# Loading a per-layer input with features on partitions by single-element DMA transfers from ScalarE's queue, in place of row loads and TensorE transposes

## What is computed

```python
for i in range(DEPTH):                      # DEPTH = 2
    f = swiglu(rmsnorm(h, g[0]), ffn_w_gate[i, 0], ffn_w_up[i, 0], ffn_w_down[i, 0])
    h = h + FFN_RES_WEIGHT * rmsnorm(f, g[1])
    m = retention(...) if i == 0 else stick_breaking(...)
    h = h + rmsnorm(m, g[3])
    f = swiglu(rmsnorm(h, g[4]), ffn_w_gate[i, 1], ffn_w_up[i, 1], ffn_w_down[i, 1])
    h = h + FFN_RES_WEIGHT * rmsnorm(f, g[5])
    gate = jax.nn.sigmoid(rmsnorm(h, g[6]) @ ple_w_gate[i])
    e = p[i] @ ple_w_proj[i]                # p[i]: (1, 256 tokens, 256 features)
    h = h + rmsnorm(gate * e, g[7])
```

## Time and profile before

| | us |
|---|---|
| Median of 3 runs | 1379.35 (1378.95 to 1379.9) |
| Span of the profiled execution | 1377.3 |
| TensorE busy | 1368.1 (99%) |
| VectorE busy | 940.4 (68%) |
| ScalarE busy | 724.2 (53%) |
| GpSimd busy | 121.1 (9%) |
| DMA engines, mean | 56.4% for SyncE's queue |

### The profile page before, as it was taken

One profiled execution on the slowest core, in us unless ns is written; L12 is line 12 of the kernel. 1 busy time (PEld: TensorE's weight loads), 2 busy tenths in 40 slices (PEclk: granted clock), 3 DMA queues, 4 the chain that ended last, 5 costly groups with the idle time before them and its releaser, 6 DMA issues.

```text
span 1377.3 us, 19699 instructions
## 1 busy us (share of the span) xinstructions
PE 1368.1 (99%) x6928; PEld 1156.3 (84%) x6928; DVE 940.4 (68%) x1128; ACT 724.2 (53%) x991; POOL 121.1 (9%) x161
## 2 busy tenths in 40 slices
PE   8999999999999999999999999999999999999999
PEld 7888888888888888888888888888888888888787
DVE  6777768667567776577777554577775676577675
ACT  6444455444454444475445366654444565545674
POOL 0111010000011110010110010011110110002100
PEclk9999999999999999999999999999999999999999
DMA  8656646555646666447567554455567456555441
GB/s 263 201 183 199 198 157 207 174 185 195 214 131 198 193 215 224 147 150 230 183 198 238 171 186 139 139 168 183 183 215 239 151 171 202 179 172 182 143 131 66
DMA packets 186960, 251.43 MB, mean 183 GB/s; under 512 B 15589, under 2 KB 115725, under 8 KB 186893
## 3 DMA queue, kind: packets, MB, share of 16 engines
q1 hardware_dynamic: 186604, 250.43, 56.4%
q10 hardware_dynamic: 288, 0.13, 0.0%
HBM read 249.45 MB, written 1.05 MB: 182 GB/s over the span
## 4 chain that ended last, share of the span: by engine, by line
PE 92%; DVE 5%; POOL 1%; ACT 1%; issue 1%; DMA 0%; POOLq 0%; DVEq 0%; ACTq 0%
PE sums L526 17%; PE sums L528 17%; PE sums L527 17%; PE sums L675 11%; PE turn L675 11%; PE sums L681 6%; PE turn L681 6%; DVE w_lo L1558 2%; PE turn L604 1%; PE turn L526 1%; PE turn L528 1%; PE turn L527 1%; POOL stat L1034 1%; DVE stat L2018 0%; DVE work L2015 0%
## 5 line engine op out<-in xcount | busy, mean ns | idle before, releaser
L1558 DVE TENSOR_TENSOR w_lo<-raw,w_hi 128x1024 fp32r<-128x1024 f32 x460 | 553.4, 1241 | 147.7 <-ACT w_hi L1105 146.3
L1105 ACT ACTIVATE w_hi<-raw 128x1024 fp32r<-128x1024 f32 x460 | 470.2, 1053 | 240.5 <-DMA raw<-in_ffn_w_up_dram 92.6
L526 PE MATMUL sums<-w_hi,x_both 128*128 128x512 f32 x608 | 241.0, 396 | 0.2 <-issue 0.2
L528 PE MATMUL sums<-w_hi,x_both 128*128 128x512 f32 x608 | 237.2, 390 | 0.0
L527 PE MATMUL sums<-w_lo,x_both 128*128 128x512 f32 x608 | 236.8, 390 | 0.0
L526 PE MATMUL sums<-w_hi,y_hi 128*128 128x512 f32 x510 | 200.3, 393 | 0.0
L528 PE MATMUL sums<-w_hi,y_lo 128*128 128x512 f32 x510 | 198.7, 390 | 0.0
L527 PE MATMUL sums<-w_lo,y_hi 128*128 128x512 f32 x510 | 198.5, 389 | 0.0
L675 PE MATMUL sums<-x_both,w_hi 128*128 128x512 f32 x640 | 153.0, 391 | 0.0
L675 PE MATMUL turn<-x_both,w_hi 128*128 128x512 f32 x640 | 152.7, 391 | 0.0
L675 PEld LDWEIGHTS turn<-x_both,w_hi 128*128 128x128 f32 x640 | 117.6, 188 | 22.8
(11 more groups left out here) (216 smaller groups left out, 1275.8 us busy)
## 6 DMA issues: line engine op xcount, KB each, us to landing
raw<-in_ffn_w_gate_dram SPq DMA_DIRECT2D x176, 256.0 KB, 3.7
raw<-in_ffn_w_up_dram SPq DMA_DIRECT2D x176, 256.0 KB, 4.5
raw<-in_ffn_w_down_dram SPq DMA_DIRECT2D x176, 256.0 KB, 3.6
raw<-in_ret_w_in_dram SPq DMA_DIRECT2D x96, 256.0 KB, 4.1
raw<-in_conv_w_in_dram SPq DMA_DIRECT2D x64, 256.0 KB, 3.7
raw<-in_attn_w_in_dram SPq DMA_DIRECT2D x64, 256.0 KB, 3.8
raw<-in_sb_w_in_dram SPq DMA_DIRECT2D x48, 256.0 KB, 3.6
raw<-in_ret_w_out_dram SPq DMA_DIRECT2D x32, 256.0 KB, 4.3
```

The source lines that it names most:

```text
L526: pe.matmul(bank[:, :], a, wh, start=(first and c == 0), stop=False, skip_group_check=True)
L528: mm = pe.matmul(bank[:, :], b, wh, start=False, stop=(last and c == SC - 1), skip_group_check=True)
L1105: act.activation(w_hi[:, n % RING].rearrange("p c n -> p (c n)"), raw[:, n % RAW].rearrange("p c n -> p (c n)"), ACT.Copy).then_inc(hi_mad ...
L1558: dve.tensor_tensor(w_lo[:, n % RING].rearrange("p c n -> p (c n)"), raw[:, n % RAW].rearrange("p c n -> p (c n)"), w_hi[:, n % RING].rear ...
```

## The change

The row loads of p (SyncE), the transposes (TensorE) and the semaphore `p_turned` are gone. ScalarE issues two transfers per layer in their place, one for each half of p's 256 features, right after the two `silu` of `ffn_in1` and `ffn_in3`. Each reads p with the token index running fastest, so that neighbouring elements are 1 KB apart in DRAM, and writes 128 partitions of 256 tokens to columns 1024 to 1535 of `work` (`HW_P`). ScalarE and VectorE then make `p_hi` and `p_lo` from `work` at the same places as before, ScalarE after a wait on `p_loaded`.

```diff
@@ sync: ffn_weights
                 load_post(f"down{f}")
-                if f % 2:
-
-                    if f == 3:
-                        sp.wait_ge(p_turned, 1)
-                    for t in range(NT):
-                        sp.dma_start(work[:, 1024 + 256 * t:1280 + 256 * t], p_in[layer, 0, t * P:(t + 1) * P, :]).then_inc(p_loaded, 16)
                 out_weights(f"down{f}", ffn_w_down[layer, half])
@@ tensor: last_hidden
-                    if f % 2:
-
-                        pe.wait_ge(p_loaded, 32 * (f // 2 + 1))
-                        for c in range(2):
-                            for t in range(NT):
-                                mm = pe.transpose(turn[1][:, c * SEQ + t * P:c * SEQ + (t + 1) * P],
-                                                  work[:, 1024 + 256 * t + c * P:1024 + 256 * t + (c + 1) * P], ident[:, :])
-                        mm.then_inc(p_turned, 1)
@@ scalar: ffn
                 for t in range(NT):
                     act.wait_ge(r_in_made, 2 * b + t + 1)
                     silu(t)
+                if f % 2:
+                    for c in range(2):
+                        act.dma_start(work[:, HW_P + c * SEQ:HW_P + (c + 1) * SEQ],
+                                      p_in[f // 2, 0, :, c * P:(c + 1) * P].rearrange("t p -> p t"), allow_slow_non_contiguous=True).then_inc(p_loaded, 16)
                 act.wait_ge(r_turned, f + 1)
...
                     if f % 2:
-                        act.wait_ge(p_turned, f // 2 + 1)
-                        act.activation(p_hi[:, :, :], turn[1][:, :].rearrange("p (c t) -> p c t", c=2),
+                        act.wait_ge(p_loaded, 32 * (f // 2 + 1))
+                        act.activation(p_hi[:, :, :], work[:, HW_P:HW_P + 512].rearrange("p (c t) -> p c t", c=2),
                                        ACT.Copy).then_inc(p_hi_made, 1)
@@ vector: ffn
-                        dve.tensor_tensor(p_lo[:, :, :], turn[1][:, :].rearrange("p (c t) -> p c t", c=2),
+                        dve.tensor_tensor(p_lo[:, :, :], work[:, HW_P:HW_P + 512].rearrange("p (c t) -> p c t", c=2),
                                           p_hi[:, :, :].bitcast(F32), ALU.subtract).then_inc(p_lo_made, 1)
```

More of the change, by code:

```diff
@@ L292, in build @@
         y_hi_made, y_lo_made = sem("y_hi_made"), sem("y_lo_made")
-        p_turned, p_hi_made, p_lo_made = sem("p_turned"), sem("p_hi_made"), sem("p_lo_made")
+        p_hi_made, p_lo_made = sem("p_hi_made"), sem("p_lo_made")
         gated, gated_sq, fg_made = sem("gated"), sem("gated_sq"), sem("fg_made")
```

## The result

The changed kernel takes 1416.04 us (median of 4 runs, 1414.69 to 1416.18) against 1379.35 before: 1.0265 times the time before, 95% interval 1.0253 to 1.0277. It is slower, as forecast, by 36.7 us where 60.5 were forecast. The profiled execution has a span of 1414.4 us, 37.1 more than before.

A forecast was written before the change was run, and what follows sets the result against it. TensorE, 1368.1 of 1377.3 us busy, was taken as the bound. Two waits of 30.7 us less 0.9 for the transposes gave +60.5 on 1379.35, so 1440 us, with a range from 1377 to 1520.

The forecast's parts named there:

- The price of an element: Each 4-byte element is one packet costing 9.2 ns of a DMA engine, so 37.7 us of every engine per layer.
- upper end of 2.5 ns over all engines: Packet pace from the stretch 12 to 13 us; at it, a layer's 65,536 elements take 162 us.
- The hold of the queue: ScalarE's queue is held behind the two issues while DMA engines take the elements: 37.7 us per layer; chance 0.50 (16 to 77).
- T: Time per layer that ScalarE's queue is held by the two issue instructions: 37.7 us, range ends 16 and 77.
- The two slopes: Issue time growth of 0.24 and 1.2 ns a row, giving 16 and 77 us per layer for 65,536 elements.
- the third row: In the opening burst a 256-row issue takes up to 0.62 us, not 0.37: taken as support for the queue being held.
- What a hold costs: TensorE waits T - 7.0 us before block 1 of ffn_in1 and ffn_in3: 30.7 us per layer.
- The clock: Nothing was taken for a slower TensorE clock after a wait of 31 us; rows showed granted clock 1.00.
- Hidden: Rival: issues take some 0.5 us, elements fit between weight packets, p is ready by 524.25; 1378.5 us, chance 0.23.
- SyncE held: Rival: SyncE's weight issues from 405 on stand, TensorE waits 24.4 us per layer at block 2; 1427 us, chance 0.10.
- p late: Rival: loading takes 162 us, ScalarE stands before p_hi, TensorE waits 29 us per layer; 1436 us, chance 0.14 including holds above 77.
- Faster: Rival: dropping row loads ahead of the down stage's weights gives 0.85 us per layer more; 1376.8 us, chance 0.03 (over 0.2%).

The follow-up runs named there:

- the kernel with the transfers far apart: The changed kernel with each layer's first transfer issued a stage earlier, in the mixer's out stage: 1378.22 us, ratio 0.9991 to the kernel before; repeated, 1378.25 us, 0.9994.
- the kernel with one transfer: The changed kernel with only the first of each layer's two transfers issued, second half of p left out: 1378.17 us, ratio 0.9993 to the kernel before.
- four transfers: The changed kernel with each layer's same elements in four transfers of 128 x 128 in place of two of 128 x 256: 1434.09 us, ratio 1.0396.
- pairs: The changed kernel with the same bytes in runs of two elements (8 bytes), half as many packets: 1397.72 us, ratio 1.0133 to the kernel before.
- behind the splits: The changed kernel with both transfers issued after `w_hi` of block 1's slots (8 to 11), 6.6 us later: 1408.88 us, ratio 1.0214.
- adjacent in DRAM: The changed kernel reading as many single elements along DRAM rows, written to every second SBUF column: 1423.44 us, ratio 1.0321 to the kernel before.

## Why the prediction was right, and where its sum was off

**What bounds the kernel: right.** TensorE set the time, and every microsecond of its waits is in the result. The waits are at the one place named, before block 1 of `ffn_in1` and `ffn_in3`; elsewhere no wait over 0.6 us is new.

**What is removed: right.** The transposes are gone from the chain, and the kernel with the transfers far apart, which has nothing else of the change on the path, stands 1.0 us below the one before, where 0.9 was worked out (by the times alone no change is possible too). No gain came from the two row loads that went.

**The price of an element: right.** 9.2 ns of one engine were worked out of two rows of the kernel before; measured are 9.4. That it came so close is in part luck, since the rounding of the rows left 7 to 11. The upper end of 2.5 ns over all engines was four times too high.

**The hold of the queue: right that there is one, wrong in which transfer is held, and the term that was mis-sized.** That ScalarE's queue is held as long as the DMA engines need for a transfer's elements is what happens, but T was set at 37.7 us, the time for *both* transfers, shared as "around 19 us each". Measured are 0.4 and 23.4 us. By the prediction's own sign, around 19 us each would have meant the forecast and half a microsecond each would have refuted it; neither is what came. A transfer doesn't hold its own issue instruction but the next transfer on its queue, and behind the second one nothing is issued on ScalarE's queue until long after. So one transfer counts: 32,768 / 16 x 9.2 ns is 18.8 us by the prediction's own price. What stood in no term is the 4 to 6 us ahead, in which the weights already under way leave the elements little room (1,847 of them in 6 us). The two slopes drawn from the issue times were no measure of either: the issue that is not held takes 0.4 us for 128 elements and for 32,768. Nor was the third row a measure: the 0.62 us of the opening burst are not the longest issue of 256 rows, since the same rows have 1.35 and 1.24 us from later stretches.

That the forecast came within 24 us of the time is partly luck. It took each issue to last as long as its own elements need. Worked out that way for the kernel with one transfer, T is 18.8 us and the loss 2 x (18.8 - 7.0) - 0.9 = 22.7 us; that kernel lost nothing. With two transfers in a row, the one that counts left a hold large enough for the same sign.

**What a hold costs: right.** T - 7.0 with T = 23.4 and 23.6 gives 16.4 and 16.6 us; TensorE waited 16.4 and 16.6. The same formula with the 32.9 us of four transfers gives 25.9, measured 26.0; with 14.68 it gives 7.7, measured 7.7.

**The clock: wrong, by 4.8 us.** It was taken at nothing since no row of the kernel before shows a fall; but no row there has a TensorE wait of such a length after the start either, so the rows could not exclude it. In all the runs with a wait the first matmuls behind it are slower, and the cost doesn't follow its length. The table has the runs whose wait stands ahead of a loop block (layer 0 / layer 1):

| Run | TensorE's wait, us | first 16 matmuls behind it, us | more than 3.65 |
|---|---|---|---|
| pairs | 7.7 / 7.4 | 6.22 / 6.80 | 2.6 / 3.2 |
| behind the splits | 13.0 / 12.0 | 6.60 / 6.49 | 3.0 / 2.8 |
| the change | 16.4 / 16.6 | 6.32 / 5.75 | 2.7 / 2.1 |
| adjacent in DRAM | layer 1: 20.0 | 6.66 | 3.0 |
| four transfers | 26.0 / 26.1 | 5.49 / 5.70 | 1.8 / 2.1 |

The same wait costs 2.7 us in one layer and 2.1 in the other. What sets the cost between 1.8 and 3.2 us was not tested.

**The sum, with the right term.** 2 x (23.5 - 7.0) + 4.8 - 0.9 = 36.9 us, where 36.7 were measured on the medians. Of the 60.5 us forecast, 28.4 went with the second transfer and the weights' share (2 x (37.7 - 23.5)), and 4.8 came back with the clock.

**The rivals.** *Hidden* was given 0.23, and it describes the single transfer exactly: 0.45 us of issue, no wait. It fails for the pair alone. The Trainium skill (DMA: Bandwidth & Descriptors, "Issuing engines are not separate DMA queues") speaks for it, and for one transfer, or for two far apart, the trace agrees with 0.39 to 0.45 us; two in a row on one queue go against it with 23.4 us. *SyncE held* is refuted for this kernel. SyncE's last issue while ScalarE is held, and its next one:

```profile
405.83 0.80 SPq L376 DMA_DIRECT2D raw<-in_ffn_w_up_dram  x1
431.04 0.38 SPq L376 DMA_DIRECT2D raw<-in_ffn_w_gate_dram  x1
```

No issue of SyncE's from 403 to 440 us takes over 0.8 us. The pause from 406.6 to 431.0 is one in which SyncE has no free slot to load, since the splits that free them stand behind ScalarE's queue; it follows from the hold. *p late* is refuted: the last p lands 69.4 us after its issue, near 474, and p_hi is made at 543.9, some 70 us later. *Faster* did not show: before and after, TensorE has no wait at the start of the down stage.

The other citations can be set against the runs as well. The Trainium skill (Perfetto Trace Analysis, "DMA Instruction — HWDGE (DVE, Sync)") has the sequencer busy until all descriptors are made: the lone transfer goes against it (0.45 us for 32,768 elements). It has the generator locked for one instruction and shared by two sequencers; SyncE held for 19.99 us while ScalarE issued in 0.40 us shows no such lock between these two. The 19 times of the Trainium skill (DMA: Bandwidth & Descriptors, "Rules for kernel authors") stand there against the DMA's own transpose; the prediction put them on row loads, which gave a T of 16 us, an estimate. Both transfers by the measured pace are 65,536 x 0.59 ns = 38.7 us of all engines.

**The weights beside the second transfer.** From 432 to 474 us the rest of the elements runs beside the loads of weights. Queues and the loads with their median time to landing:

```profile
q1 hardware_dynamic: 8870, 8.56, 78.2%
q10 hardware_dynamic: 27595, 0.11, 44.4%
...
raw<-in_ffn_w_gate_dram SPq DMA_DIRECT2D x17, 256.0 KB, 6.2
raw<-in_ffn_w_up_dram SPq DMA_DIRECT2D x17, 256.0 KB, 6.9
```

In the kernel before, the same two loads land in 3.8 and 4.7 us there. They land 2.2 to 2.4 us later, and TensorE still waits for none, since the splits are some slots ahead. That the elements fit into the free time of the DMA engines was right, and so was that a microsecond or two of landing is hidden.

## What to carry to other kernels

Where one load is made of many small packets, count packets and not bytes, and ask what transfer comes next on the same queue: that one, whatever it is, is held until the packets are handed out, and its engine with it. One such transfer on a queue that issues nothing else is nearly free, and a second one should come only when the first is gone, or on another queue; splitting it into more pieces makes it worse. When a row shows a median that lies between two very different values, look at the instructions one by one before spreading the cost evenly over them.

## What the runs showed of the hardware

- An issue of 32,768 single-element packets with nothing in its way takes 0.37 to 0.47 us (0.56 with the elements adjacent in DRAM). The next transfer on the queue, also an ordinary one of 256 rows, is held 18.0 to 24.3 us behind it (26.8 with the elements adjacent in DRAM). The other queue isn't held. The smallest transfer ahead that was tried has 16,384 packets; from how many on a hold shows wasn't tested.
- The pace is 0.53 to 0.59 ns per packet over 16 engines, about the same for 4 and 8 bytes, and 0.67 ns for elements that are adjacent in DRAM. With weights under way it is far lower at first: 1,847 elements in 6 us.
- Behind a wait of TensorE of 5.1 us, the shortest that the experiments added, its matmuls already came 0.43 us apart for 6.3 us, and 0.23 us after that. Behind waits of 7.4 to 26.1 us the first 16 matmuls took 1.8 to 3.2 us more, and the longest wait has not the highest price.
